# Expert outputs kept in PSUM and summed by one-hot matmuls, in place of an accumulating scatter to DRAM

## The reference

```
h = rmsnorm(x, norm2_g) * (1 + scale2(c)) + shift2(c)
logits = h @ w_router + b_router              # 32 experts
top_val, top_idx = top_k(logits, 4); top_w = softmax(top_val)
for e in range(32):
    hh   = h @ w_expert_in[e] + b_expert_in[e]              # 1024 -> 2048
    gate = min(hh[:, :1024], 7); lin = clip(hh[:, 1024:], -7, 7)
    act  = (lin + 1) * gate * sigmoid(1.702 * gate)
    y   += comb[:, e] * (act @ w_expert_out[e] + b_expert_out[e])   # 1024 -> 1024
x = x + gate2(c) * y
out = rmsnorm(x, final_norm_g)
```

## Time and profile before

| | |
|---|---|
| median of 3 runs | 1531.92 us (1530.77 to 1532.19) |
| the profiled execution | 1529.73 us, of which 1528.0 us span |
| PE matmul busy | 1259.7 us (82%) |
| DVE, ACT, POOL busy | 356.3, 307.9, 183.5 us |
| mean granted TensorE clock | 0.915 |
| DVE, the gathered rows `xg`, 128x256 (L1526) | 49 times, mean 425 ns |
| ACT, a side of an output, 32x256 (L1164) | 196 times, mean 467 ns |
| moved by DMA | 534.38 MB, mean 350 GB/s |
| critical chain | PE 56%, DMA 40% |

### The profile page before, as it was taken

How to read it: one execution, slowest core, us unless ns; L and a number is a source line. 1 busy time by engine, 2 the same in 40 slices (tenths; PEclk the granted TensorE clock), 3 DMA queues, 4 the chain that set the end, 5 groups by cost and what they waited for, 6 DMA issues and landing times.

```text
span 1528.0 us, 27699 instructions
## 1 busy us (share of the span) xinstructions
PE 1259.7 (82%) x10935; PEld 692.7 (45%) x10936; DVE 356.3 (23%) x756; ACT 307.9 (20%) x638; POOL 183.5 (12%) x300
## 2 busy tenths in 40 slices
PE   6999999999999789999954698496969666954694
PEld 3777887767887434444421243132423222421241
DVE  1023113333631322222211122121222112211123
ACT  3100122442100222222211122121212111211123
POOL 0240100100180001111000011000100000100010
PEclk9999999999999899999987699797989888987697
DMA  9876734999555388799999999999999999999994
GB/s 367 303 286 227 267 111 149 386 371 402 184 179 226 139 342 338 285 419 421 415 427 427 425 412 423 425 419 426 415 418 411 429 423 416 417 429 426 422 411 170
DMA packets 76681, 534.38 MB, mean 350 GB/s; under 512 B 6428, under 2 KB 7540, under 8 KB 49793
## 3 DMA queue, kind: packets, MB, share of 16 engines
q1 hardware_dynamic: 67330, 503.47, 80.5%
q0 software_dynamic: 8928, 29.54, 6.0%
q10 hardware_dynamic: 391, 0.93, 0.2%
HBM read 508.38 MB, written 28.09 MB: 351 GB/s over the span
## 4 chain that ended last, share of the span: by engine, by line
PE 56%; DMA 40%; DVE 2%; SPq 1%; issue 1%; ACT 0%; DVEq 0%; ACTq 0%; POOL 0%; POOLq 0%
DMA ring<-in_w_expert_in_dram 21%; PE ps L754 16%; PE ps L922 12%; DMA moe_ring<-in_w_expert_out_dram 11%; PE ps L946 9%; DMA moe_ring<-in_w_expert_in_dram 5%; PE ps L511 2%; PE ps L891 2%; PE ps L796 2%; PE ps L837 2%; PE ps L803 2%; PE ps L783 2%; DMA ring<-in_w_in_dram 1%; DMA ring<-in_w_ada_dram 1%; PE ps L558 1%; PE ps L637 1%
## 5 line engine op out<-in xcount | busy, mean ns | idle before, releaser
L922 PE MATMUL ps<-ring,xgT 128*32 128x512 f32 x2352 | 318.7, 664 | 179.0 <-DMA ring<-in_w_expert_in_dram 178.5
L754 PE MATMUL ps<-hT,ring 128*128 128x264 f32 x1152 | 268.8, 391 | 6.1 <-DMA ring<-in_w_in_dram 4.7
L754 PEld LDWEIGHTS ps<-hT,ring 128*128 128x128 f32 x1152 | 218.5, 192 | 59.4 <-issue 14.6
L922 PEld LDWEIGHTS ps<-ring,xgT 128*32 128x32 f32 x2352 | 66.2, 116 | 318.3 <-DMA ring<-in_w_expert_in_dram 185.5
L946 PE MATMUL ps<-moe_ring,actT 128*32 128x256 f32 x3136 | 181.7, 380 | 4.7 <-DMA moe_ring<-in_w_expert_out_dram 4.2
L1526 DVE TENSOR_TENSOR xg<-ps,sh_q 128x256 f32<-128x256 f32 x49 | 20.8, 425 | 554.9 <-PE ps L891 554.9
L1164 ACT ACTIVATE ostage<-ps,slots_w 32x256 f32<-32x256 f32 x196 | 91.6, 467 | 285.9 <-PE ps L946 284.1
L946 PEld LDWEIGHTS ps<-moe_ring,actT 128*32 128x32 f32 x3136 | 99.3, 110 | 86.1 <-issue 18.0
L922 PE MATMUL ps<-moe_ring,xgT 128*32 128x512 f32 x784 | 93.7, 595 | 21.3 <-DMA moe_ring<-in_w_expert_in_dram 21.3
L891 PE MATMUL ps<-rows,picked 128*32 128x256 f32 (+1 forms) x1200 | 81.8, 386 | 1.3 <-DVE picked L1481 1.3
L1156 ACT COPY actT<-ps 128x256 f32<-128x256 f32 x49 | 18.3, 373 | 306.7 <-PE ps L511 306.7
(11 more groups left out here) (285 smaller groups left out, 1135.3 us busy)
## 6 DMA issues: line engine op xcount, KB each, us to landing
ring<-in_w_expert_in_dram SPq DMA_DIRECT2D x96, 2048.0 KB, 12.3
moe_ring<-in_w_expert_out_dram SPq DMA_DIRECT2D x64, 2048.0 KB, 12.0
moe_ring<-in_w_expert_in_dram SPq DMA_DIRECT2D x32, 2048.0 KB
ring<-in_w_in_dram SPq DMA_DIRECT2D x18, 2048.0 KB, 12.1
ring<-in_w_ada_dram SPq DMA_DIRECT2D x12, 2048.0 KB, 8.7
ring<-in_state_ret_dram SPq DMA_DIRECT2D x8, 1024.0 KB, 10.8
vslot<-in_state_ret_dram SPq DMA_DIRECT2D x8, 1024.0 KB, 10.8
out_dram<-ring POOLq DMA_DIRECT2D x8, 1024.0 KB, 9.1
```

Source lines behind the costliest of these rows:

```text
L754: mm = nc.tensor.matmul(ps[:, j, 0:T], ring[s][:, k, j * P:(j + 1) * P], hT[:, k, :], start=(k == 0), stop=(k == KC - 1))
L922: mm = nc.tensor.matmul(side(0, g), xgT[:, a, j * SLOTS:(j + 1) * SLOTS], w[:, a, g * COL:(g + 1) * COL], start=False, stop=(j == 3 and a ...
```

## The change

The expert outputs don't leave the core. Four PSUM banks (4 to 7, `ACC + g`) hold the running output: bank 4+g has columns 256g to 256g+255 of x for the first 128 tokens in its left half and for the second 128 tokens in its right half. `sums_begun` sets them to the residual stream, by a product with zeros that opens the bank and then four products with `xT` as the stationary operand. After each item, `combine` adds 32 slots to them: the stationary operand is a one-hot matrix from slot to token (`slot_rows`, built by DVE in `spread_slots`), the moving one is the item's output times its routing weight and gate2 (`gated`, from `gate_outward`). Side g is on partitions 32g to 32g+31, so that the four matmuls of one half of the tokens use the four row groups of the array, each with its own bank.

The 8 samples have gates of their own. One more product with `slot_samples` sums their rows side by side into the second half of bank 2, and DVE adds this to `sample_sum` for every item; at the end it is gated and added on PE.

ACT now takes an item's output in one activation of 128x256. The indirect DMA, its clearing, the copy of slot numbers, the reload and the row-wise additions are gone; the squares and the last scaling read PSUM. To free the banks, the gathered rows and the slot data move to bank 1, the activations' transposes to bank 3, and the counts to bank 6.

```diff
+        def summed(t):
+            return ps[:, ACC:ACC + SIDES, t * QUARTER:(t + 1) * QUARTER] if t < 2 else ps[0:TS, 0:2, :]
@@ SP, end
-            sp.wait_ge(rows_free, items + 1)
-            sp.sem_inc(paced, 1)
-            for t, (t0, n) in enumerate(TILES):
-                sp.dma_start(y_in[t][0:n], moe_rows[t0:t0 + n]).then_inc(rows_in[t], 16)
@@ PE
+            def sums_begun():
+                for g in range(SIDES):
+                    nc.tensor.matmul(ps[:, ACC + g, :], zero_h[:, 0:P], zero_h[:], start=True, stop=False)
+                    for t in range(2):
+                        for k in range(2):
+                            nc.tensor.matmul(ps[:, ACC + g, t * QUARTER + k * P:t * QUARTER + (k + 1) * P], xT[:, 2 * g + k, t * P:(t + 1) * P], ident, start=False, stop=False)
+                nc.tensor.matmul(ps[0:SIDES * TS, 2, QUARTER:2 * QUARTER], slot_samples[:], out_rows[:], start=True, stop=True).then_inc(samples_summed, 1)
+
+            def combine(q, last=False):
+                pe.wait_ge(slots_spread, q + 2)
+                pe.wait_ge(out_gated, q + 2)
+                pe.sem_inc(paced, 1)
+                for t in range(2):
+                    for g in range(SIDES):
+                        slots = slice(SLOTS * g, SLOTS * (g + 1))
+                        mm = nc.tensor.matmul(ps[:, ACC + g, t * QUARTER:(t + 1) * QUARTER], slot_rows[slots, t * P:(t + 1) * P], gated[slots], start=False, stop=last and t == 1)
+                if last:
+                    mm.then_inc(combined, 1)
+                nc.tensor.matmul(ps[0:SIDES * TS, 2, QUARTER:2 * QUARTER], slot_samples[:], out_rows[:], start=True, stop=True).then_inc(samples_summed, 1)
@@ PE, outward
+                pe.wait_ge(samples_added, q + 2)
+                pe.sem_inc(paced, 1)
@@ PE, the loop over the items
             turn_gathered(1)
+            sums_begun()
             with pe.Fori(1, items) as q:
...
                 turn_gathered(q + 1)
+                combine(q - 1)
                 pe.wait_ge(slots_taken, SLOT_STEPS * q + SLOT_STEPS)
                 pick(q + 1, after)
@@ PE, end
-            rows_turned_back(0, 3)
+            for h in range(2):
+                nc.tensor.matmul(ps[0:TS, h, :], zero_h[:, 0:TS], zero_h[:], start=True, stop=False)
+            for k in range(KC):
+                nc.tensor.matmul(ps[0:TS, k // 4, (k % 4) * P:(k % 4 + 1) * P], xT[:, k, TP:T], ident, start=False, stop=False)
             turn_hidden(items - 1)
-            outward(items - 1, last, True)
+            outward(items - 1, last)
+            combine(items - 1, True)
+            pe.wait_ge(sample_gated, 1)
+            for g in range(SIDES):
+                mm = nc.tensor.matmul(ps[0:TS, g // 2, (g % 2) * QUARTER:(g % 2 + 1) * QUARTER], ident[0:SIDES * TS, TS * g:TS * (g + 1)], sample_sum[:], start=False, stop=(g % 2 == 1))
+            mm.then_inc(combined, 1)
@@ ACT
-                for g in range(SIDES):
-                    side = slice(SLOTS * g, SLOTS * (g + 1))
-                    mv = nc.scalar.activation(ostage[:, g * QUARTER:(g + 1) * QUARTER], ps[side, 2, 0:QUARTER], ACT.Copy, scale=slots_w[side, bass.ds(q, 1)])
-                mv.then_inc(eo_taken, 1)
+                nc.scalar.activation(out_rows[:], ps[:, 2, 0:QUARTER], ACT.Copy, scale=slots_w[:, bass.ds(q, 1)]).then_inc(eo_taken, 1)
@@ DVE
+            def spread_slots(q):
+                dve.wait_ge(slots_taken, SLOT_STEPS * q + SLOT_STEPS)
+                for g in range(SIDES):
+                    side = slice(SLOTS * g, SLOTS * (g + 1))
+                    ts(slot_samples[side, TS * g:TS * (g + 1)], const("iota")[side, 0:TS], float(TP), slots_f[side, bass.ds(q, 1)], ALU.add, ALU.is_equal)
+                ts(slot_rows[:, 0:P], const("iota"), slots_f[:, bass.ds(q, 1)], None, ALU.is_equal)
+                ts(slot_rows[:, P:TP], const("iota"), float(P), slots_f[:, bass.ds(q, 1)], ALU.add, ALU.is_equal).then_inc(slots_spread, 1)
+
+            def add_samples(q):
+                dve.wait_ge(samples_summed, q + 1)
+                dve.wait_ge(samples_added, q + 1)
+                tt(sample_sum[:], sample_sum[:], ps[0:SIDES * TS, 2, QUARTER:2 * QUARTER], ALU.add).then_inc(samples_added, 1)
+
+            def gate_outward(q):
+                dve.wait_ge(eo_taken, q + 1)
+                tt(gated[:], out_rows[:], gate_side[:], ALU.mult).then_inc(out_gated, 1)
@@ DVE, the loop
                 choose(q + 1, after)
+                spread_slots(q)
                 take_gathered(q + 1)
+                gate_outward(q)
...
+                take_slots(q + 1, bass.ds(q + 1, 1), bass.ds(q + 2, 1))
+                add_samples(q)
@@ DVE, while the dues are awaited
+            step(nc.vector.memset(slot_samples[:], 0.0))
+            step(nc.vector.memset(slots_f[:, 0:1], -1.0))
+            step(nc.vector.memset(out_rows[:], 0.0))
+            step(nc.vector.memset(sample_sum[:], 0.0))
+            step(nc.vector.memset(zero_h[:], 0.0))
@@ POOL
-            step(nc.gpsimd.memset(b_full[:, 0:11 * P], 0.0))
-            for i in range(2):
-                pool.dma_start(moe_rows..., b_full[:, 0:11 * P]).then_inc(moe_cleared, 16)
+            for g in range(SIDES):
+                pool.dma_start(gate_side[SLOTS * g:SLOTS * (g + 1)], kept_rows[1, 0:1, g * QUARTER:(g + 1) * QUARTER].broadcast_to([SLOTS, QUARTER])).then_inc(gates_in, 16)
+                pool.dma_start(gate_sample[TS * g:TS * (g + 1)], kept_rows[1, 1:NB, g * QUARTER:(g + 1) * QUARTER]).then_inc(gates_in, 16)
```

More of the change, by code:

```diff
@@ L217, in trunk_kernel @@
         glu_s = new("glu_s", [2 * SLOTS, COL])
-        ostage = new("ostage", [SLOTS, D])
         assert top[0] <= h_at
@@ L856, in _ @@
             for t in range(3):
-                mm = nc.tensor.matmul(ps[0:E, 1, COUNTS:COUNTS + 1], mask_h[:, t, :], ones_h[:, 0:1], start=(t == 0), stop=(t == 2))
+                mm = nc.tensor.matmul(ps[0:E, 6, COUNTS:COUNTS + 1], mask_h[:, t, :], ones_h[:, 0:1], start=(t == 0), stop=(t == 2))
             mm.then_inc(counted, 1)
@@ L862, in ends_counted @@
                 for last, table in ((False, "upper"), (True, "ident")):
-                    nc.tensor.matmul(ps[:, 1, ENDS:ENDS + E], item_nb[:], const(table, E)[:, 0:E], start=not last, stop=last)
+                    nc.tensor.matmul(ps[:, 6, ENDS:ENDS + E], item_nb[:], const(table, E)[:, 0:E], start=not last, stop=last)
                 for last, table in ((False, "upper"), (True, "ident")):
-                    mm = nc.tensor.matmul(ps[0:E, 1, END:END + 1], const(table, E)[:, 0:E], item_nb[:, 0:1], start=not last, stop=last)
+                    mm = nc.tensor.matmul(ps[0:E, 6, END:END + 1], const(table, E)[:, 0:E], item_nb[:, 0:1], start=not last, stop=last)
                 mm.then_inc(counted, 1)
@@ L890, in gather @@
                     for g in range(SIDES):
-                        mm = nc.tensor.matmul(side(6, g)[:, 0:QUARTER], picked[0:n, t, 0:SLOTS], rows[0:n, t, g * QUARTER:(g + 1) * QUARTER],
+                        mm = nc.tensor.matmul(side(1, g)[:, 0:QUARTER], picked[0:n, t, 0:SLOTS], rows[0:n, t, g * QUARTER:(g + 1) * QUARTER],
                                               start=(t == 0), stop=(t == 2))
@@ L1190, in square_rows @@
                 n = TILES[t][1]
-                act_e.wait_ge(y_added, t + 1)
-                nc.scalar.activation(y_sq[t][0:n], y_out[t][0:n], ACT.Square, accum_out=small[0:n, 2 + t:3 + t]).then_inc(y_squared, 1)
+                act_e.wait_ge(combined, (1, 1, 2)[t])
+                nc.scalar.activation(cut_rows(y_sq[t][0:n], t), summed(t), ACT.Square, accum_out=small[0:n, 2 + t:3 + t]).then_inc(y_squared, 1)
             def take_root(t):
@@ L1703, in _ @@
                 bias_column(bias_sel, after, bias_sel_ready)
-                scatter(q - 1, here)
-            scatter(items - 1, None)
+                pool.wait_ge(eo_taken, q + 1)
+                pool.sem_inc(paced, 1)
+                bias_column(bias_out, here, out_bias_ready)
 _INS = ["x_prompt", "x_sample", "c_prompt", "c_sample", "state_pool", "state_ret", "w_ada", "b_ada", "norm1_g", "w_in",
```

150 lines of the change are left out of this document (54 added, 96 removed).

## The result

| | before | after |
|---|---|---|
| median of the runs side by side | 1532.05 us (4 runs) | 1576.52 us (4 runs, 1572.64 to 1579.33) |
| profiled execution, its span | 1529.73, 1528.0 | 1579.33, 1577.5 |
| PE busy | 1259.7 us | 1348.9 us |
| chain of waits, share of PE, DMA, issue | 56%, 40%, 1% | 70%, 25%, 3% |

The ratio is 1.0290, 95% interval 1.0272 to 1.0309. The forecast was 1526.2, with a range of 1513 to 1552, and faster.

A forecast was written before the change was run, and what follows sets the result against it. PE was taken to bound three-item experts, the loads one-item experts, with two-item experts nearly level. Front +15.2, experts 7 to 31 -10.4 and tail -10.5 gave -5.7: 1531.9 to 1526.2 us, range 1513 to 1552.

The forecast's parts named there:

- c: PE work added to each item by combine and the sample product: 1.8 us, bounds 1.3 to 4.4.
- Rivals 1 to 3: In combine: staggered first loads, 1537 us (chance 0.12); loads wholly in line, 1551.5 (0.18); eight matmuls in line, 1610 (0.07).
- rival 4: In combine, shape changes overlap with neighbours: 1.3 us an item, whole kernel 1513 us; chance 0.18.
- The item's period: Front items on PE: outward products 14.30 us apart before, 16.1 us after with the new work.
- the step on starvation: Experts 7 to 31, loads issued too late: 1.2 us lost over five lone two-item experts, 6.1 over two pairs.
- rival 2: In combine, weight loads wholly in line, 16 x 0.11 us: +25 us, 1551.5 us; chance 0.18.
- Front: Items 0 to 14, taken as PE-bound: 19.0 us later at item 14, less 3.8 back, +15.2 us.
- 3.8 us of backlog: After item 14 the loads have no backlog: expert 8's chunk 0 comes at 18.8 us, not 22.6.
- Experts 7 to 31: After the front: 17.7 us saved by dropping scatters, less starvation of the loads, together -10.4 us.
- The scatter's 17.7: Experts 7 to 31: 34 items' scatters go, each costing the DMAs 0.52 us, -17.7 us.
- Tail: From the last product to the kernel's end: -11.4 us, or -9.7 with PE at 1.2 GHz; taken as -10.5.
- C: Experiments' theory: combine's eight short products, about 33 ns an instruction, use up PE's lead (issuing ahead of execution).

The follow-up runs named there:

- e5: The kernel before without the scatter to DRAM and its wait, so the sum of expert outputs is left out: 1507.35 us, ratio to before 0.9827.
- f2_loads: The changed kernel with two of three register loads moved from the head of PE's loop to around the outward product: 1537.58 us, ratio to before 1.0037.
- g1_pieces: The changed kernel with two register loads moved and the sample product cut into four 64-column products: 1529.46 us, ratio to before 0.9976.
- f1: The changed kernel without combine's eight products (except for the last item), its waits, increment and sample product kept: 1512.02 us, ratio to before 0.9867.
- g2: The changed kernel with four of combine's eight products (all eight for the last item): 1554.75 us, ratio to before 1.0152.
- g3: The changed kernel with all eight combine products reading rows 0 to 31, one row group: 1696.65 us, ratio to before 1.106.
- h1: The changed kernel with one register load (`after`) moved from the loop's head to behind the outward product: 1550.48 us, ratio to before 1.0106.

## Why the prediction was wrong

The spans, cut at outward products. "Two" are the 18 intervals in which experts of two items are at work (with outward product 0 as the first: 18 to 22, 24 to 26, 27 to 31, 32 to 34, 36 to 38, 39 to 41, 45 to 47); "one" the 15 others from item 14 on; the last interval stands alone. Each figure is a sum of differences between starts in the timelines.

| us | before | no scatter (e5) | f2_loads | after | g1_pieces |
|---|---|---|---|---|---|
| start to item 14 | 760.1 | 760.9 | 777.8 | 796.1 | 772.2 |
| "two", 18 intervals | 270.7 | 267.6 | 290.7 | 311.5 | 287.7 |
| "one", 15 intervals | 452.8 | 438.6 | 433.3 | 437.4 | 434.6 |
| last interval | 13.0 | 12.5 | 15.1 | 15.1 | 14.8 |
| last outward product to the end | 31.6 | 26.6 | 16.9 | 17.3 | 16.4 |
| span | 1528.0 | 1506.3 | 1533.8 | 1577.5 | 1525.7 |

1. **The work of an item, c: right.** Forecast 1.8 us, bounds 1.3 to 4.4. Without the stall the item is 15.91 us (f2_loads) against 14.30, so c is 1.61. The eight products take 1.08 us where the sum had 1.23 (0.13 + 0.11 + 0.86 + 0.13), the sample product 0.55 for 0.56. The eight products lie beside each other. Rivals 1 to 3, which priced them higher, are not what happened, nor is rival 4 with its 1.3.
2. **The item's period: the step that failed.** "Then the item of 14.30 + c" takes the period to be the work. It was work + 1.15 us of a stall (17.06 - 15.91), a term that the sum does not have. The parts were at hand: the row [0.63 <-issue] in the earlier trace rows says that PE's issuing needs 3.55 us from the start of `hidden(3)` (1007.69) to the bias products (1011.24), where PE has 2.9 us to do. I read it as idle to subtract (0.63 of the 0.93, and the 5.83 - 0.63, in the step on starvation) and did not ask what hides it elsewhere and whether the change leaves that cover. It puts 32 short instructions just there. The price: f2_loads to after is 18.3 us at item 14, 20.9 in "two", 4.1 in "one", 43.7 us of span (39 by the medians). The sentence "Spacing of 16.9 or more makes rival 2" would have named the wrong cause: the spacing was 17.06 with `combine` at its forecast price.
3. **Front.** Opening of the sums 6.0 us as forecast (545.81 to 551.83). Item 14 forecast at 779.1; 777.8 without the stall, 796.1 with it. That 779.1 and 777.8 lie so close is in part luck: outward product 0 came at 555.0 and not at 553.7, and the lower c took 2.6 us back. Of the 3.8 us of backlog that were to come back, 2.5 did: expert 8's chunk 0 came 20.1 us behind item 14's outward product in f2_loads (797.91), where the forecast had 18.8 and the kernel before 22.6.
4. **Experts 7 to 31: a second step that failed,** smaller. Forecast -10.4 there, and -3.8 of backlog: -14.2 from item 14 on. Measured +27.7 (311.5 + 437.4 + 15.1 against 270.7 + 452.8 + 13.0), and +2.7 without the stall. The scatter's 17.7 is right as a sum. What was too small is "0.24 lost" for a lone expert of two items and 3.0 for a pair: f2_loads against e5_noscatter is +20.3 where these give 7.3. By the table it is +23.1 in "two", -5.3 in "one" and +2.6 in the last interval. The step counted the time in which the DMAs would have nothing to do. The windows from item 14 to the last item but one (e5, f2, after) show full or nearly full shares, but a lower rate:

```profile
760.91:1467.16 706.25, 513.64 (x5680) 208.61 (x5676) 128.06 (x330) 126.11 (x264) 18.63 (x99) 0.85 1.01 428
```

```profile
777.80:1501.78 723.98, 571.36 (x6274) 240.60 (x6270) 196.25 (x594) 76.73 (x165) 13.68 (x66) 0.87 1.00 417
```

```profile
796.07:1545.02 748.95, 575.50 (x6274) 242.74 (x6270) 195.41 (x594) 76.81 (x165) 14.74 (x66) 0.87 0.97 404
```

   The bytes are the same (302 MB each), so the stretch is as long as the rate is low. In f2_loads the issues of chunks 4 and 5 around an expert of two items are 31.8 us apart (1171.90 and 1203.71), twice the item, and can't come at 29.36:

```profile
1171.90 2.06 SPq L483 DMA_DIRECT2D moe_ring<-in_w_expert_out_dram  x2
...
1203.71 2.05 SPq L483 DMA_DIRECT2D moe_ring<-in_w_expert_out_dram  x2
```

   The share at 1.00 hid it; the GB/s beside it did not. What makes the rate fall while the share stays at 1.00 is not shown.
5. **Tail: right.** From the end of the last product to the end of the kernel 13.1 us (1560.77 + 3.66 to 1577.5) against 24.6 before: 11.5 less, forecast 10.5. The first square comes 2.5 us behind that end, where the forecast (4.7 behind the start of a half of 1.93) had 2.8. The other 2.8 of the 14.3 in the table lie ahead of that end, where PE before waited 0.99 us for a chunk and turned rows back.

Sum without the stall: 17.7 + 2.7 - 14.7 = +5.8 us of span (f2_loads), against -5.7. The stall adds 43.7.

**What stays open.** That the eight short products bring the idle is shown (f1, g2, g3), and that the loads at the loop's head are what must be covered (f2, h1). How the lead is lost in them is not: half of the products gave 0.77 us, all 1.07, none 0, which is no straight line. C's price of 33 ns an instruction can't be the whole of it: at that price the 32 instructions are issued in the 1.07 us that they run, and would leave the lead as it was, where they brought 1.07 us of idle. E, that these products are not queued behind the work before them, stays open beside C. The Trainium skill (Advanced Engine Details and Errata, section Engine Queue Depths) gives TensorE a queue of 64 instructions. No run here shows that depth, and alone it would not give the idle: the last 48 instructions before the loop's turn, `combine`, the sample product and `pick`, are worth 2.4 us, more than the estimated 1.9 to 2.0 us of the turn.

## What to carry to other kernels

An idle put down to "issue" ahead of a loop's first product shows by how much the lead fell short of what the loop's turn needs; look for it in items where PE had waited, and ask whether the work that hides it elsewhere stays. Here short products just before the loop's turn, together with register loads at its head, made a stall of it in each pass: move the loads behind long work first (two lines, 39 us here), and move them even when the kernel at hand gains nothing by it, if PE's work there is about to change. Price a load-bound stretch by its GB/s, not by its share alone.

## What the runs showed of the hardware

- One register load from SBUF (`after`) cost PE's issuing 0.68 us at the loop's head (moved: idle 1.07 to 0.39 us).
- Four row groups of 32 rows, 256 fp32 columns, into four banks: 8 products in 1.08 us, against 3.65 in one row group.
- Four products of 64 columns in four column groups take 0.25 us, one of 256 columns 0.55.
- The granted clock in the front was 1.00 with PE busy without a gap (f2_loads) and 0.99 with 1.07 us of idle in 17. With the eight products in one row group it was 0.87, though PE had no gap there either; behind 3.7 us of them the next `hidden` ran at 0.51 (609.36 to 612.84).
- An accumulating scatter of 32 rows of 4 KB cost 0.94 us between experts of one item, where the loads set the time, and 0.17 in experts of two (14.1 us for 15, 3.0 for 18).
